# Fifteen projections of the second block as seven products of quarters, the value projection moved ahead of the delta rule and through DRAM

## The reference, cut to what matters

```python
h = rms_norm_2(x, norm_gain) * (1.0 + scale) + shift
(q_a, k_a, v_a, z_a, b_a, a_a, q_b, k_b, v_b, z_b, gl_a, gl_b) = split_cols(h @ w_in, IN_SPLITS)
# delta side: causal conv of q_a, k_a, v_a, the chunked gated delta rule (8 heads, 8 chunks of 64 tokens)
o_a = rms_norm_2(o_a, gdn_norm_gain) * silu(z_a);      y_gdn = o_a @ w_branch_gdn
# window side: normed q_b (16 heads of 64), normed k_b and v_b (4 heads), window of 128 tokens, bias and sinks
y_swa = (o_b * silu(z_b)) @ w_branch_swa
mixed = sigmoid(gl_a) * y_gdn + sigmoid(gl_b) * y_swa
x = x + gate * (mixed @ w_out)
```

## Time and profile before

| what | us |
|---|---|
| median of 3 runs (4425.51 to 4427.81) | 4427.38 |
| the profiled execution's own time | 4427.27 |
| its span, first to last instruction | 4425.5 |

### The profile page before, as it was taken

The page is one execution under the profiler, slowest core; times in us unless marked ns, Lnnn a source line. Parts: engine busy times, 40 slices in busy tenths (PEclk is TensorE's granted clock), DMA queues, the critical chain, the costliest instruction groups (busy, mean ns, idle before and its releaser), DMA issues.

```text
span 4425.5 us, 36819 instructions
## 1 busy us (share of the span) xinstructions
PE 4250.6 (96%) x14170; PEld 2404.6 (54%) x14170; DVE 2146.5 (49%) x3815; ACT 848.4 (19%) x1447; POOL 486.9 (11%) x803
## 2 busy tenths in 40 slices
PE   6899999999999999999999999999999999999999
PEld 3565544444456554444478345555555644447788
DVE  5576436664525563457565533333422234435543
ACT  1222101131012220112301312121311123330000
POOL 0133111111202331111110000000000001100000
PEclk7899999999999999999999999999999999999999
DMA  8533333234532233332444221112121333333333
GB/s 325 173 114 105 119 115 128 95 123 150 173 135 90 94 120 105 127 114 90 149 159 128 97 76 57 54 51 67 57 67 50 99 94 121 125 100 122 110 100 100
DMA packets 368477, 495.34 MB, mean 112 GB/s; under 512 B 44091, under 2 KB 278062, under 8 KB 367790
## 3 DMA queue, kind: packets, MB, share of 16 engines
q1 hardware_dynamic: 289840, 340.16, 23.6%
q0 software_dynamic: 37632, 122.71, 8.9%
q10 hardware_dynamic: 40830, 30.11, 2.2%
HBM read 460.42 MB, written 32.51 MB: 111 GB/s over the span
## 4 chain that ended last, share of the span: by engine, by line
PE 86%; DVE 11%; ACT 1%; DMA 1%; issue 1%; ACTq 0%; POOL 0%; SPq 0%; DVEq 0%
PE bank L108 83%; PE bank L111 2%; DVE tring L117 2%; DVE tring L123 2%; DVE tring L132 1%; DVE dring L120 1%; DVE dring L117 1%; DMA side<-in_w_ada 1%; DVE tring L120 1%; ACT tring L114 1%; DVE bank L117 0%; DMA yaT<-in_w_ada 0%; DVE wring L117 0%; DVE sring L138 0%; ACT L114 0%
## 5 line engine op out<-in xcount | busy, mean ns | idle before, releaser
L108 PE MATMUL bank<-region_b,wring 128*128 128x512 f32 (+2 forms) x4448 | 1886.1, 575 | 24.7 <-DVE wring L117 16.0
L108 PEld LDWEIGHTS bank<-region_b,wring 128*128 128x128 f32 (+1 forms) x4448 | 829.8, 192 | 875.1 <-issue 829.9
L108 PE MATMUL bank<-region_a,wring 128*128 128x512 f32 (+1 forms) x1920 | 772.2, 555 | 0.0
L108 PEld LDWEIGHTS bank<-region_a,wring 128*128 128x128 f32 x1920 | 360.2, 192 | 347.2 <-issue 336.0
L147 POOL DMA_DIRECT2D side<-in_w_ada x384 | 209.0, 545 | 1468.7 <-DVE tring L123 938.8
L123 DVE SCALAR_TENSOR_TENSOR tring<-side,cact,tring 128x512 f32<-128x512 f32 x360 | 305.2, 848 | 76.8 <-DMA side<-in_w_ada 40.2
L114 ACT ACT_TABLE_LOAD x196 | 251.5, 1283 | 403.2 <-DVE sring L120 283.7
L108 PE MATMUL bank<-wring,region_b 128*128 128x512 f32 (+1 forms) x640 | 266.6, 573 | 0.5 <-ACT region_b L114 0.5
L132 DVE RECIPROCAL tring<-tring 128x512 f32<-128x512 f32 x54 | 180.8, 3348 | 107.6 <-ACT tring L114 107.6
L108 PE MATMUL bank<-wring,region_a 128*128 128x512 f32 x512 | 226.5, 600 | 6.0 <-ACT region_a L114 6.0
L108 PEld LDWEIGHTS bank<-wring,region_b 128*128 128x128 f32 x640 | 150.4, 239 | 112.7 <-issue 85.0
(11 more groups left out here) (268 smaller groups left out, 4061.9 us busy)
## 6 DMA issues: line engine op xcount, KB each, us to landing
wring<-in_w_in SPq DMA_DIRECT2D x180, 1024.0 KB, 5.3
side<-in_w_ada POOLq DMA_DIRECT2D x384, 256.0 KB, 3.2
wring<-in_w_out SPq DMA_DIRECT2D x48, 1024.0 KB, 7.6
yaT<-in_w_ada SPq DMA_DIRECT2D x16, 1024.0 KB, 8.0
wring<-in_w_glu SPq DMA_DIRECT2D x16, 1024.0 KB, 7.5
gring<-in_w_ada POOLq DMA_DIRECT2D x64, 256.0 KB, 3.1
tring<-x_saved SPq DMA_DIRECT2D x48, 256.0 KB, 3.2
SS<-in_w_ada SPq DMA_DIRECT2D x8, 1024.0 KB, 7.7
```

The source lines that it names most:

```text
L108: return self.e.matmul(*a, **k) if self.e else self
```

## The change: what it does

Cut to its core. The k, q and z_b jobs and the six gate jobs beside the windows use fast through two_job; the conv, z_a and ten gate jobs beside the delta rule stay dense. h gets quarter sums (h_parts): three of them in region_a's first 12 tiles, made ahead of the v job; the fourth in place of a quarter of h, by quarter_last, once the fence "delta" is passed. The v job moves ahead of the first value conv job; VectorE copies its tiles to temporaries, ScalarE stores them to v_saved, and v_fetch on SyncE brings them into qkv2 after the fence "delta", in front of the k weights. region_a's last four tiles (zslots) hold z_a and the output of a delta head; heads 0 to 3 are stored to oa_saved by GpSimd, and oa_fetch on SyncE brings them to tiles 8 to 11 after the fence "window". z_b and ob lie in a new buffer obm. fold uses two parts of a temporary in place of three beside s3 and adds product 1 to bank x in fold 0, for which product 7 waits. s3 has one place; in block two it is the table that only the delta rule needed. mix takes the window branch first. The modulation's ring has three places. Some constants of the first two blocks get a table of their own (const_one), loaded by a second DMA. In add_gated of the second block the two steps quarter_rest come after product 4 of the first job.

```diff
+        const_one = sb("const_one", [P, split - cut], first)
...
+        s3_window = Room([const_two[:, 0:HT * P].rearrange("p (k n) -> p k n", k=HT)], ("delta",))
         delta_mem.close()
         band, k2, q2 = sb("band", [P, 16, 256], two), sb("k2", [P, 2, T], two), sb("q2", [P, 2, T], two)
-        gring = sb("gring", [P, 4, T], two)
+        gring, obm = sb("gring", [P, 2, T], two), sb("obm", [P, HT, T], two)
...
-        mixedT = sb("mixedT", [P, 4, HT, 256], mixed_mem)
-        s3_last = Room([sb(f"s3_last{i}", [P, HT + 6, P], mixed_mem) for i in range(2)])
+        mixedT = sb("mixedT", [P, 2, HT, 256], mixed_mem)
+        s3_last = Room([sb("s3_last", [P, HT, P], mixed_mem)])
...
+        wide_slots = Room([gring[:, i, :].unsqueeze(1) for i in range(2)] + [const_two[:, hot:hot + T].unsqueeze(1)])
+        zslots = Room([regions[0][:, 12 + i, :] for i in range(4)])
...
+            temps.take("fold", jid)
+            for p, then in ((1, ()), (2, (("set_by",), ("w_sum", 2))), (4, (("w_sum", 4),)), (6, ()), (5, (("fold", 0),)),
                             (7, (("fold", 1),)), (3, (("fold", 2),))):
                 do("seventh", jid, p)
-                for name, *n in late:
+                for name, *n in then:
                     do(name, jid, *n)
+                if p == 4:
+                    for step in late:
+                        do(*step)
...
+        def two_job(n0, use, *args):
+
+            return Dense(w_two, KT, n0, 256, False, None, h_parts.ready, use, (2, *args), h_parts, s3_window)
...
+            if h < 4:
+                do("oa_store", h)
+                zslots.give("za2", h)
...
-            yield from dense(layer_dense(2, w_two, OFF["kb"], "keep_k2"), after)
-            yield from dense(layer_dense(2, w_two, OFF["vb"], "keep_v2", tokens="blocks"))
+            yield from fast(two_job(OFF["kb"], "keep_k2"), after)
             yield from settle()
...
-            yield from dense(layer_dense(2, w_two, OFF["qb"] + kv * 256, "keep_q2", kv), after)
-            yield from dense(layer_dense(2, w_two, OFF["zb"] + kv * 256, "keep_zb", kv))
+            yield from fast(two_job(OFF["qb"] + kv * 256, "keep_q2", kv), after)
+            yield from fast(two_job(OFF["zb"] + kv * 256, "keep_zb", kv))
...
+                if seven:
+                    yield from fast(two_job(OFF[name] + n0, "save_gate", name, n0 // P))
+                else:
+                    yield from dense(layer_dense(2, w_two, OFF[name] + n0, "save_gate", name, n0 // P))
...
+            yield from branch_gates(2, False)
...
+            do("oa_fetch")
             quarter(ob, 0, 4)
+            for s in (oa, ob):
+                s.chunk.update((k, 0) for k in range(4))
...
-                run_all(fast(Dense(wa, HT, n0, 256, False, None, oa.ready, "mix_first", (n,), oa, s3_last)))
-                run_all(fast(Dense(wb, HT, n0, 256, False, None, ob.ready, "mix_second", (n,), ob, s3_last)))
+                run_all(fast(Dense(wb, HT, n0, 256, False, None, ob.ready, "mix_first", (n,), ob, s3_last), None, () if n0 else
+                             (("quarter_rest", ob, 0, 4), ("quarter_sums", oa, 0, 4), ("quarter_rest", oa, 0, 4))))
+                run_all(fast(Dense(wa, HT, n0, 256, False, None, oa.ready, "mix_second", (n,), oa, s3_last)))
                 if n >= HT:
                     quarter(mixed_parts, n - HT, 2)
+                    do("quarter_rest", mixed_parts, n - HT, 2)
...
+        h_parts = Split("h", KT, lambda r, k, n: regions[1][:, HT * r + k:HT * r + k + n, :], lambda k: [h_ready.of(2, k)],
+                        [regions[1][:, 0:HT, 256:512], *(pairs_of(regions[0][:, 4 * i:4 * i + 4, :]) for i in range(3))],
+                        lambda: [x_stored.of(2)], {})
+        for k in range(0, HT, 4):
+            quarter(h_parts, k, 4)
+            do("quarter_rest", h_parts, k, 4)
+        for j in range(TT):
+            temps.take("vb", j)
+        run_all(dense(layer_dense(2, w_two, OFF["vb"], "keep_v2", tokens="blocks")))
+        for j in range(TT):
+            do("save_v2", j)
+            temps.give("vb", j)
...
-        interleave(delta_pair(GH - 2), branch_gates(4), 32 / 36)
+        interleave(delta_pair(GH - 2), branch_gates(4, False), 32 / 36)
         do("fence", "delta")
+        for k in range(0, HT, 4):
+            do("quarter_last", h_parts, k, 4)
         do("band_fetch")
+        do("v_fetch")
         run_all(kv_products())
         run_all(swa_products(0))
         behind.append(modulation(GATE_OF[2]))
-        carried[:] = [1.6, 0.0]
+        carried[:] = [1.9, 0.0]
         for kv in range(1, 4):
-            interleave(window(kv - 1), beside_window(kv), 24 / 16)
-        interleave(window(3), branch_gates(3), 24 / 16)
+            interleave(window(kv - 1), beside_window(kv), 21 / 16)
+        interleave(window(3), branch_gates(3), 21 / 16)
         finish_behind(0)
         do("fence", "window")
         mixed_parts = Split("mixed", KT, lambda r, k, n: mixed[:, HT * r + k:HT * r + k + n, :], lambda k: [taken_d.of("mixed", k)],
...
-                if p == 3:
+                if p == 7:
                     pe.wait_ge(*folded.of(jid, 0))
...
-                    dve.tensor_tensor(six, z[:, 256:512], one, AD).then_inc(*folded.up(jid, 0))
+                    dve.tensor_tensor(two, z[:, 256:512], one, AD).then_inc(*d_step.up())
+                    dve.tensor_tensor(x[:, 0:256], x[:, 0:256], one, AD).then_inc(*folded.up(jid, 0))
                 elif n == 1:
                     dve.wait_ge(*folded.of(jid, 0))
-                    dve.tensor_tensor(five, y[:, 256:512], six, AD).then_inc(*folded.up(jid, 1))
+                    dve.tensor_tensor(one, y[:, 256:512], two, AD).then_inc(*folded.up(jid, 1))
                 elif n == 2:
                     dve.wait_ge(*folded.of(jid, 1))
-                    dve.tensor_tensor(six, x[:, 256:512], six, AD).then_inc(*d_step.up())
-                    dve.tensor_tensor(x[:, 0:256], x[:, 0:256], one, AD).then_inc(*d_step.up())
+                    dve.tensor_tensor(two, x[:, 256:512], two, AD).then_inc(*d_step.up())
                     own()
                     both = y[:, :].rearrange("p (h t) -> p h t", h=2)
-                    dve.tensor_tensor(both, both, six.unsqueeze(1).broadcast_to([P, 2, 256]), AD).then_inc(*folded.up(jid, 2))
+                    dve.tensor_tensor(both, both, two.unsqueeze(1).broadcast_to([P, 2, 256]), AD).then_inc(*folded.up(jid, 2))
                 else:
                     dve.wait_ge(*folded.of(jid, 2))
-                    dve.tensor_tensor(x[:, 256:512], z[:, 0:256], five, AD).then_inc(*folded.up(jid, 3))
+                    dve.tensor_tensor(x[:, 256:512], z[:, 0:256], one, AD).then_inc(*folded.up(jid, 3))
                     banks.leave((jid, "z"), dve.mine())
-                    jobs[jid].s3.leave(("s3", jid), dve.mine())
+                    temps.leave(("fold", jid), dve.mine())
+
...
+            def quarter_rest(s, k0, n):
+                _, b12, _, b22 = quarters_of(s, k0, n)
+                dve.tensor_tensor(s.sums[2][:, k0:k0 + n, :], b22, b12, SU).then_inc(*quarters_summed.up(s.name, 2, k0))
+
+            def quarter_last(s, k0, n):
+                b11, b12, _, _ = quarters_of(s, k0, n)
+                room(passed("delta"))
+                dve.wait_ge(*quarters_summed.of(s.name, 2, k0))
+                dve.tensor_tensor(s.sums[0][:, k0:k0 + n, :], b12, b11, SU).then_inc(*quarters_summed.up(s.name, 0, k0))
...
+                room(temps.clear("vb", j))
+                dve.tensor_copy(temps.at("vb", j)[:, 0:256], banks.at(jid, j)[:, 0:256]).then_inc(*taken_d.up("vb", j))
...
+            def save_v2(j):
+                act.wait_ge(*taken_d.of("vb", j))
+                act.dma_start(v_saved[j], temps.at("vb", j)[:, 0:256]).then_inc(*stored("vb", j).landing("vb", j))
...
+            def oa_store(h):
+                pool.wait_ge(*delta_d.of("oa", h))
+                pool.dma_start(oa_saved[h], zslots.at("za2", h)).then_inc(*oa_out[h].landing(h))
+                zslots.leave(("za2", h), oa_out[h].of(h))
...
+            def oa_fetch():
+                room(passed("window"))
+                for s in oa_out:
+                    sp.wait_ge(*s.all())
+                sp.dma_start(regions[0][:, 8:12, :], oa_saved.rearrange("h p t -> p h t")).then_inc(*oa_in.landing())
+
+            def v_fetch():
+                v4 = qkv2[1][:, 0:4, :].rearrange("p j (h n d) -> p j h n d", h=4, n=2)
+                room(passed("delta"))
+                for j in range(TT):
+                    sp.wait_ge(*stored("vb", j).of("vb", j))
+                    for n in range(2):
+                        sp.dma_start(v4[:, j, :, n, :], v_saved[j].rearrange("p (h d) -> p h d", h=4)).then_inc(*v_in.landing())
...
+            sp.dma_start(const[:, :], d["const"][:, 0:cut]).then_inc(*const_in.landing())
+            sp.dma_start(const_one[:, :], d["const"][:, cut:split]).then_inc(*const_in.landing())
```

(5 more changed lines are left out.)

153 lines of the change are left out of this document (85 added, 68 removed).

## The result

The changed kernel takes 4442.27 us (median of seven runs, 4436.84 to 4444.92), the kernel before 4426.07 us (seven, 4423.56 to 4427.89): a ratio of 1.0034, interval 1.0022 to 1.0045. That is 16.2 us more, where 5 less were forecast, and just above the top of the range (4441).

A forecast was written before the change was run, and what follows sets the result against it. TensorE, busy 96% of the span, was taken to bound the kernel. Terms -49.1 + 19.6 + 5.8 + 17 + 6.2 - 2.5 - 2.4 + 0.4 = -5.0 gave 4422 us from 4427.38; range 4405 to 4441.

The forecast's parts named there:

- Step 1: Fifteen jobs (k, four q, four z_b, six gates) change form: -49.1 us, if TensorE never waits.
- Step 2: Delta fence: v_fetch ahead of the k weights idles TensorE 17.4 us, slow restart 2.2: +19.6 (16 to 25).
- Step 3: Seam from k to q: waits for ScalarE's root and weight sums behind two reciprocals, +5.8 us (2 to 9).
- Step 4: Twelve jobs beside the windows: VectorE's load loses 5 us in three windows, 2 in the last, +17 (4 to 40).
- Step 5: Window fence before mix: oa_fetch and gate tiles precede the first branch weights, product 7 later, +6.2 us (2 to 11).
- Step 6: Small terms: shorter fold 2 in mix -2.5 us, layer 1's output projection -2.4, two-part constant load +0.4.
- D: Slower: VectorE paces the windows from about 95 us busy plus waits; loss 40 instead of 17, 4445 us; chance 0.20.
- B: TensorE is fed beside the windows: loss 4 instead of 17, delta stall at its lower bound, 4405 us; chance 0.30.
- C: Delta fence: small v pieces go at half of 358 GB/s, +3 us, 4425 us; chance 0.10.

The follow-up runs named there:

- e8: Changed kernel with e5, e6 and e7 together and no settle (emptying of the norm units) between k and q jobs: 4385.51 us, ratio 0.9912.
- e11: e10 with the fold in three places, product 3 instead of product 7 waiting for fold 0: 4371.52 us, ratio 0.9878.
- e7: Changed kernel with the norm unit of the second q tile started two products later: 4424.07 us, one run.
- e10: e8 with both q norm units one product later: 4374.04 us, ratio 0.9884.
- e5: Changed kernel with oa_fetch behind the first mix job's gate tiles and branch weights in SyncE's order: 4427.65 us.
- e9: e8 with the fold in three places, the add into bank x back in fold 2, product 3 waiting for fold 0: 4381.2 us, ratio 0.99.
- e4: Changed kernel with the modulation's sums beside the windows on 64 of 512 columns, same instruction count and order: 4435.15 us.
- e2: Changed kernel with v stored doubled, rows of 2 KB, fetched by four DMAs in place of eight: 4433.93 us.
- e1: Changed kernel with v_fetch moved behind the k job's loads in SyncE's order: 4415.97 us, ratio 0.9978.
- e6: Changed kernel without v's trip through memory, the v job behind the delta fence, VectorE writing v in place: 4411.37 us, ratio 0.9967.
- e3: Changed kernel with q and z_b jobs of the later head pairs dense again, gates by seven products, filler rate 23/16: 4432.7 us.

## Why the prediction was wrong, step by step

**Step 1, the jobs' price: right.** 16 instructions take 3.62 us back to back. In e8 nothing waits between the last gate tile and the first scores, and that stretch is 10.0 us shorter than before (102.1 for 112.1) with three of the jobs in it (9.8). In e11, where little waits, the four windows win 36.1 of their 39.2.

**Step 2, the stall at the delta fence: right in kind, mis-sized.** 24.1 of wait and 2.8 of slow restart (9.88 for 7.07) are 26.9 for 19.6. Against its lower bound of 14.2 the wait is 9.9 longer: 1.2 since TensorE was done earlier than I had set, 3.3 for SyncE's issues (0.83 for a v piece and not 0.43: I took a weight block's issue as the price of a DMA of another shape), and 5.75 for a landing of 11.05 where 5.3 was the median, less 0.4 since SyncE went earlier. While the block was on its way the DMA engines were full (0.95 to 1.17), with v, the band, the later blocks and w_ada beside it. I had allowed 3.2 over that bound, and the upper one, 22, was passed as well.

**Step 3, the seam: mis-sized a little.** 2.97 and 3.75 of waits and 1.8 of slow clock (5.41 for 3.62), 8.5 for 5.8: the clock's 1.8 had no term.

**Step 4, the windows: the step that failed.** Loss predicted 17 (5, 5, 5 and 2), measured 26.9: the windows would have been 90.6, 90.5, 92.2 and 87.6 without waits, and were 99.7, 100.4, 99.4 and 88.3. The text named VectorE's uneven load at q and z_b and then put a flat 5 on it, and named fold 0 as the wait that would end last. The runs showed another: two reciprocals 6 us apart, with weight sums between and the softening of scores behind (6.7 of waits, 4.3 the longest), and then the clock, about 2 us per window (5.56 for 3.62 in the second), which step 4 had no term for though step 2 had. e7 and e10 show that it is the place: same VectorE work, 3 to 4 us less per window and then, in e10, 6.6 to 7.9.

**Step 5, mix: right in kind, a little short.** 12.7 for a forecast idle of 11.8, and product 7 of the first job 8.0 us later for 6.2. e5 shows that it need not have been paid.

**Step 6: right in kind, one size off.** Layer 1's opening 2.3 for 2.4. The shorter fold 2 saved 1.8 us of waits for 2.5, as four of the passes had only 0.19 to give (e9, which has the long one again, waits in mix as before did: 0.19 or 3.05, 3.08, where e8 waits 0 or 2.7). With them went slow restarts of 6.0 us, which had no term. The two misses of steps 5 and 6 are of opposite sign, and that their sum came out near the forecast is luck.

**The rivals.** D (VectorE paces the windows) came nearest in time, but not by its mechanism: its point, 95 us of busy time and waits per window, is a sum, and e4 cut that sum by 9 and left most of the waits. B was wrong for the change and right about what could be had: in e11 TensorE is fed, with VectorE at 69. C named the same stall for another reason: e2 leaves 2.2 us at most for small pieces and their many issues, against 7.3 that the stall went beyond the forecast.

**What stays open.** Of the median's 16.2 us, the two profiled executions show 10.1 and 11.8 (before's profiled execution is itself 1.2 above its median). Four of the seven runs took 4442.27 to 4444.92, and none of those was profiled; their granted clock is 0.974 to 0.975 against 0.976. More slow restarts after the same waits, as between e8 and e10, would fit; in the changed kernel itself it was not shown. Nor was it tried which part of the landing of 11.05 us is v's, the band's, the later weight blocks' or w_ada's; e1 and e6 show only that the stall goes when v is not ahead of the weights.

## What to carry to other kernels

When a removed matmul uncovers a fence, look at what stands behind the fence in each issuing queue: one line moved (e1) turned the loss into a gain. A step's load on the helper engine is to be counted by place: list what TensorE waits for next behind the longest instruction there, and give each wait its slow restart besides. Undo by halves (e3), then move before you remove (e7 against e4): that told place from sum in two kernels.

## What had not been expected of the hardware

- A SyncE DMA of 128 partitions by four pieces of 256 B took 0.80 to 0.84 us of the queue to issue (eight in 6.43 and 6.68), one of 2 KB rows 0.44.
- A 1 MB weight block issued beside 1 MB of v and the band tiles came after 11.05 us, and after 13.8 where the v issues ahead of it were quicker: a quicker queue gave little, with the DMA engines' busy share at 0.87 to 1.17 all the while in both.
- Waits of 3 to 4 us inside a busy stretch had a price of their own, 5.41 to 5.56 us for 16 instructions that take 3.62 otherwise, at a granted clock of 0.97 over the window; where the waits were down to 1.3 us (e10) the clock stayed at 1.00. After waits of 2.7 us in mix the price was there in 8 of 33 cases (5.15 to 5.41) and not in the others (3.72), after 3.05 us in 8 of 9; so with 0.35 us less of a wait often went another 1.4 to 2.9 us. Once it was there after 2.11 us (e1, 5.41).
